# Pooling and gating in the turned layout in the front of a decoder step

## The chip, the cores and the metric

The kernel runs on one core of a Trainium2 chip. The metric is the device time of one execution in microseconds (us). All tensors and all matmuls are float32. In the trace a float32 matmul stands as two passes, so a line that issues 24 matmuls shows 48 records.

## The reference, cut to what matters

One layer of a decoder step over 1024 prompt tokens and 64 sample tokens (8 sequences of 8), width 1024. The front of the layer is what the change touches:

```python
h = rmsnorm(x, norm1_g)
proj = h @ w_in                                   # 1024 -> u 512 | v 512 | p 512
uv = gelu(proj[..., :1024]); u, v = uv[..., :512], layernorm(uv[..., 512:])
p = proj[..., 1024:]
z = einsum('hts,bcshd->bcthd', tril(ws), v) + bs  # 4 heads, chunks of 128 tokens
ya = u * z
# 4 groups of 128 channels, windows w = 2, 4, 8, 16 over the tokens
pooled = (sum of the last w rows of p) / min(pos + 1, w) - p
yb = (pooled @ b_w[g]) * b_scale
x = x + concat(ya, yb) @ w_out
```

Behind it come a second norm, a router, and a mixture of 32 experts (top 2 of 8 in one of 4 groups), each with three matrices of 2 MB, and a last norm. The last 15 rows of p of the prompt are an output of their own.

## The kernel before

**Tiles.** The tokens are cut into nine tiles: tile 0 (called "first"), tiles 1 to 7 ("mid"), and tile 8 of 64 rows ("sample"). `pipeline` calls `step(i, cur, prev, pprev, nxt)` on every engine: step i projects, gates and pools tile i, finishes the second norm and the router's logits of tile i-1, places tile i-2 in the experts' tables, and prepares the turned input `hT` of tile i+1. Steps 2 to 6 are a hardware loop, the others are written out. Each engine runs its instructions in the order of the program, and semaphores join the engines.

**TensorE in one mid step**, in its order: two small rank products (L1166, L1167); the projections v, u and p, each 8 matmuls with `hT` stationary and 512 columns of `w_in` moving, into banks 2, 3 and 4 (L1182); z, four products over the chunk (L1193, bank 5); the pooling, for each group a product with the matrix `band` and one with `band_prev` over the tile before, kept in `ptail` (L1205, bank 6); the turn of the next tile's normed input `xn` (L1131 called from L1212, banks 0 and 1); the turn of the gated `ya` (L1131 called from L1216, bank 5); the product with `b_w` (L1221); the turn of `xn2` of the tile before (called from L1228, again banks 0 and 1, so it waits until `hT` has been taken); the first half of the output projection (L1239), the router's logits (L1247), and the second half (L1255). The first half waits for `yaT_ready` and `ybT_ready`, the two halves of the turned input `yT`.

**VectorE in a mid step**: residual adds (L908, L911), placing, two norms, the layer norm of v (L929 to L944), the gate (L953: z + bias, times u, one instruction for each head), the copy of p into `ptail` (L957), `hT` of the next tile (L822), the scaled yb half of `yT` (L964), the turned h2 (L972), and the router's choice on small tiles (L833 to L853). **ScalarE**: two squares, GELU of v and of u, the copy of p, the copy of the pooled half to `poolT` (L716), and the copy of the turned `ya` into `yT` (L720).

**Behind the front** the expert phase runs 32 blocks of 64 to 96 rows. Its up-products (L1285) are already in the form in which a piece of 64 weight columns is stationary, the turned tokens move, and two such pieces fill the two halves of the array and of the PSUM partitions; its down-products are L1306.

Of the kernel before, what the change touches and what calls it, by code (L numbers as in the profile page):

```python
# [14 lines left out]
P = 128  # L15
D = 1024
SEQ = 1024
NS = 64
DEC, DSEQ = 8, 8
T = SEQ + NS  # L20
NT = SEQ // P + 1
KD = D // P
AW = 512
# [3 lines left out]
TAIL = 32  # L27
# [20 lines left out]
NOWHERE = 1 << 14  # L48
LASTSLOT = NE * (REG - P) + NE - 1
# [25 lines left out]
def build(nc, x_prompt, x_sample, state_pool, norm1_g, w_in, a_norm_g, a_norm_b, ws_sht, bs_th,  # L75
# [4 lines left out]
    with ctx:  # L80
# [20 lines left out]
        vg, p, ya, ptail = [big[:, third + (NT + 1) * D + i * AW:third + (NT + 1) * D + (i + 1) * AW] for i in range(4)]  # L101
# [7 lines left out]
        band = bands[:, 0:AW].rearrange("p (g n) -> p g n", n=P)  # L109
        band_prev = bands[:, AW:D].rearrange("p (g n) -> p g n", n=P)  # L110

        ident = sb("ident", [P, P])
        band_first = sb("band_first", [P, GROUPS, P])
# [6 lines left out]
        bst = sb("bst", [P, HEADS])  # L120
# [3 lines left out]
        gf = sb("gf", [P, D])  # L124
        bsc = sb("bsc", [P, GROUPS])
# [59 lines left out]
        turn_int = band_first[:, 3, 0:NE].bitcast(I32)  # L185
        turn_row = sb("turn_row", [P, NE])
        slot_row, slot_int, pick = band_first[:, 0, :], band_first[:, 1, :].bitcast(I32), band_first[:, 2, :]
# [23 lines left out]
        state_moved = sem("state_moved")  # L211
# [20 lines left out]
        ptail_ready = sem("ptail_ready")  # L232
# [20 lines left out]
        p7_stored = sem("p7_stored")  # L253
# [5 lines left out]
        caps_set = sem("caps_set")  # L259
# [18 lines left out]
        turns_numbered = sem("turns_numbered")  # L278
        turn_row_made = sem("turn_row_made")
        table_late = sem("table_late")  # L280
        h2_late = sem("h2_late")
        slots_numbered = sem("slots_numbered")
# [73 lines left out]
        def _(sp):  # L356
# [26 lines left out]
            for q in range(4):  # L383
# [4 lines left out]
            load(bst[:, :], bs_th)  # L388
            load(band_first[:, :, :], c_band_first)
# [4 lines left out]
                         w_out[0, 0:AW, :].rearrange("(p k) n -> p k n", k=HEADS)).then_inc(in_wout, 16)  # L394
            sp.dma_start(wout[:, HEADS:KD, :],
                         w_out[0, AW:D, :].rearrange("(g d) n -> d g n", g=GROUPS)).then_inc(in_wout, 16)
            load_late(band[:, :, :], c_band)
            load_late(band_prev[:, :, :], c_band_prev)
# [9 lines left out]
            load_late(gf[:, :], normf_g.partition_broadcast(P))  # L408
            sp.wait_ge(zeroed, 1)
            for b in range(DEC):  # L410
# [7 lines left out]
                         state_pool[0, :, DSEQ:STATE, :]).then_inc(state_moved, 16)  # L418
# [25 lines left out]
            sp.wait_ge(p_copied, LAST)  # L444
            sp.dma_start(pool_p[0, 0], p[P - STATE:P, :]).then_inc(p7_stored, 16)
# [6 lines left out]
            sp.wait_ge(v_ready, NT)  # L452
            sp.dma_start(v_s[0].rearrange("b s c -> (b s) c"), v[0:NS, :]).then_inc(outs, 16)
            sp.wait_ge(proj_p, NT)
            for n in range(CH):
                sp.dma_start(chunk_dst(n, n), chunk_src(FIRST, n)).then_inc(chunk_in[n], 16)
            store_h2(LAST, NS)
            sp.wait_ge(outs, 16 * (DEC + 1))
# [23 lines left out]
            sp.wait_ge(yaT_done, NT)  # L482
            sp.wait_ge(ptail_ready, NT)
# [19 lines left out]
            sp.wait_ge(state_moved, 16)  # L503
# [13 lines left out]
        def _(pool):  # L517
            pool.memset(wst_s[:, :, :], 0.0).then_inc(zeroed, 1)
            pool.iota(filler.rearrange("p (q c) -> p q c", c=2), pattern=[[1, NE * REG // P], [0, 2]], base=0,
# [7 lines left out]
            pool.memset(caps[:, FIRST:NE], float(NE * CAP)).then_inc(caps_set, 1)  # L527
            for lo, hi, caps_of in CLASSES + ((FINAL, FINAL + 1, FINAL_CAPS),):
                for h in range(lo, hi):
                    for s, cap in enumerate(caps_of):  # L530
                        at = SETS * (h - 1) + s
                        pool.memset(caps[:, at:at + 1], float(NE * cap)).then_inc(caps_set, 1)
# [25 lines left out]
            for j in range(LAST):  # L558
                if j == 1:
                    pool.wait_ge(pooled, 1)  # L560
                    pool.iota(turn_int, pattern=[[1, NE]], base=0, channel_multiplier=0).then_inc(turns_numbered, 1)
                    pool.iota(slot_int.rearrange("p (i w) -> p i w", w=WAYS), pattern=[[NE, P // WAYS], [NE * P // WAYS, WAYS]],
                              base=FIRST, channel_multiplier=0).then_inc(slots_numbered, 1)
# [17 lines left out]
            pool.wait_ge(filled, 9)  # L581
# [833 lines left out]
```

## Time and profile before

| | |
|---|---|
| median of 3 runs | 977.61 us (976.02 to 978.34) |
| profiled execution, its own time | 981.23 us |
| its span | 979.6 us |
| TensorE busy over the span | 900.6 us, 92% |
| VectorE busy | 257.5 us, 26% |
| ScalarE busy | 110.0 us, 11% |
| mean granted TensorE clock | 0.963 of full |

The front takes about 380 us of the span, the experts run from about 404 us to 943 us, and the last norm follows. Busy time says which engine works most; which one ends last at a given place has to be read from the order of the records there.

### The profile page before, as it was taken

What the parts mean: (1) busy time and instruction counts of PE and PEld (TensorE: products, weight loads), DVE (VectorE), ACT (ScalarE), POOL (GpSimd) and SP (SyncE); (2) the same over time, 40 slices, a digit from 0 to 9 for tenths busy, and PEclk for the clock granted to TensorE, in tenths of its full rate; (3) what the DMA queues carried; (4) which work ended last, traced back from release to release, by engine and by line L of the source; (5) the groups of instructions that cost most, each with busy time, mean ns of one, the idle gap of its engine ahead of it and who ended that gap; (6) DMA issues with size and microseconds to landing.
All of it is one profiled execution on the core that took longest, in us unless ns stands there. A gap on an engine that the chain in (4) does not pass through costs nothing.

```text
span 979.6 us, 24674 instructions
## 1 busy us (share of the span) xinstructions
PE 900.6 (92%) x10538; PEld 596.2 (61%) x10538; DVE 257.5 (26%) x779; ACT 110.0 (11%) x173; POOL 155.4 (16%) x260
## 2 busy tenths in 40 slices
PE   4999999999999995799999999999999999989940
PEld 2545555454554563767868686868686768567630
DVE  1443454625445356150010101010101010100106
ACT  0210111101111011101001000001010101001013
POOL 1000100000000000211213131312122313113110
PEclk9999999999999997699999999999999999979985
DMA  8870200201021027799999999999999999999738
GB/s 340 275 292 1 87 31 12 86 0 43 8 78 44 3 91 286 301 399 392 353 393 404 393 407 391 408 389 409 389 408 391 402 394 401 398 405 400 270 70 321
DMA packets 57440, 258.70 MB, mean 264 GB/s; under 512 B 10809, under 2 KB 11889, under 8 KB 40356
## 3 DMA queue, kind: packets, MB, share of 16 engines
q1 hardware_dynamic: 47484, 238.51, 60.7%
q0 software_dynamic: 9264, 19.36, 8.1%
q8 instruction: 41, 0.67, 0.3%
q10 hardware_dynamic: 640, 0.07, 0.1%
q14 instruction: 11, 0.09, 0.0%
HBM read 240.86 MB, written 25.04 MB: 271 GB/s over the span
## 4 chain that ended last, share of the span: by engine, by line
PE 54%; issue 3%; DVE 2%; DMA 2%; DVEq 0%; ACT 0%; SPq 0%; POOLq 0%; POOL 0%
PE ps L1285 31%; PE ps L1306 19%; PE ps L1131 3%; DVE big L1115 1%; DMA big<-x_rows 1%; DMA x_rows<-xn,sidx 0%; PE ps L1319 0%; DMA xg<-h_rows,oidx 0%; PE ps L1314 0%; DVE ssf L806 0%; DVE ssf L805 0%; DVE ssf L808 0%; DVEq L80 0%; ACT junk L784 0%; DMA slot_table<-ids,dest 0%
## 5 line engine op out<-in xcount | busy, mean ns | idle before, releaser
L1285 PEld LDWEIGHTS ps<-hT,big 128*64 128x64 f32 x8192 | 299.5, 139 | 41.1 <-issue 39.1
L1285 PE MATMUL ps<-hT,big 128*64 128x80 f32 (+2 forms) x8192 | 308.6, 236 | 13.0 <-issue 10.7
L1306 PE MATMUL ps<-big,poolT 128*80 128x512 f32 (+2 forms) x512 | 191.2, 594 | 0.6 <-issue 0.6
L1182 PE MATMUL ps<-big,hT 128*128 128x512 f32 x384 | 168.9, 599 | 4.3 <-DMA big<-in_w_in 2.9
L1182 PEld LDWEIGHTS ps<-big,hT 128*128 128x128 f32 x384 | 72.8, 192 | 95.0 <-issue 88.0
L1306 PEld LDWEIGHTS ps<-big,poolT 128*80 128x80 f32 (+2 forms) x512 | 64.5, 149 | 103.1 <-issue 102.0
L1079 DVE TENSOR_TENSOR poolT<-u,ps 128x320 f32<-128x320 f32 (+2 forms) x32 | 15.5, 486 | 421.7 <-PE ps L1285 421.7
L577 POOL DMA_INDIRECT x_rows<-xn,sidx x22 | 32.9, 1495 | 274.1 <-ACT xn L763 253.1
L553 POOL DMA_INDIRECT slot_table<-ids,dest x18 | 18.9, 1052 | 305.4 <-DVE dest L879 263.3
L1239 PE MATMUL ps<-big 128*128 128x512 f32 x128 | 56.4, 593 | 0.9 <-DVE big L964 0.9
L1255 PE MATMUL ps<-big 128*128 128x512 f32 x128 | 57.0, 598 | 0.0
L763 ACT ACTIVATE xn<-ps,gslot 80x1024 f32<-80x1024 f32 (+1 forms) x21 | 23.3, 1110 | 259.1 <-PE ps L1306 259.1
L1239 PEld LDWEIGHTS ps<-big 128*128 128x128 f32 x128 | 23.7, 190 | 28.0 <-issue 27.8
L1255 PEld LDWEIGHTS ps<-big 128*128 128x128 f32 x128 | 23.7, 190 | 27.6 <-issue 27.3
L572 POOL DMA_INDIRECT gslot<-gate_rows,pidx x32 | 32.2, 1007 | 21.3 <-POOL sidx L623 14.0
L996 DVE TENSOR_TENSOR hT<-ps,g2t 128x768 f32<-128x768 f32 (+1 forms) x32 | 28.0, 875 | 27.6 <-PE ps L1131 18.3
L1131 PE MATMUL ps<-ident,xn 128*128 128x128 f32 (+1 forms) x144 | 21.3, 297 | 13.2 <-DVE xn L817 8.4
L577 POOL DMA_INDIRECT x_rows<-bands,sidx x10 | 14.6, 1460 | 89.2 <-DVE bands L1086 76.0
L754 ACT ACTIVATE u<-ps 128x320 f32<-128x320 f32 (+2 forms) x32 | 13.9, 435 | 125.2 <-PE ps L1285 125.2
L1131 PEld LDWEIGHTS ps<-ident,xn 128*128 128x128 f32 (+1 forms) x144 | 18.6, 196 | 14.5 <-issue 9.6
L953 DVE SCALAR_TENSOR_TENSOR big<-ps,bst,u 128x128 f32<-128x128 f32 x32 | 9.0, 345 | 67.6 <-PE ps L1193 67.6
L695 ACT ACTIVATE xn<-big 128x1024 f32 (+2 forms) x9 | 9.5, 1057 | 150.3 <-DVE big L911 150.3
(184 smaller groups left out, 561.2 us busy)
## 6 DMA issues: line engine op xcount, KB each, us to landing
big<-in_exp_w SPq DMA_DIRECT2D x192, 1024.0 KB
big<-in_w_in SPq DMA_DIRECT2D x4, 1536.0 KB, 13.4
big<-in_w_out SPq DMA_DIRECT2D x2, 2048.0 KB, 14.4
x_rows<-big SPq DMA_DIRECT2D x8, 512.0 KB
h_rows<-xn SPq DMA_DIRECT2D x8, 512.0 KB, 2.9
big<-x_rows SPq DMA_DIRECT2D x8, 512.0 KB, 7.2
out_y_prompt<-big SPq DMA_DIRECT2D x8, 512.0 KB, 2.8
big<-in_x_prompt SPq DMA_DIRECT2D x1, 3072.0 KB, 11.3
```

Source lines behind the costliest of these rows:

```text
L553: pool.indirect_dma_start(slot_table, bass.IndirectOffsetOnAxis(ap=dest[0:m, j, c:c + 1], axis=0), ids[0:m, j, c, :], None, bounds_check=N ...
L572: pool.indirect_dma_start(dst, None, gate_rows, bass.IndirectOffsetOnAxis(ap=idx.bitcast(U32), axis=0), bounds_check=last_pair, oob_is_err ...
L577: pool.indirect_dma_start(x3_rows, bass.IndirectOffsetOnAxis(ap=idx.bitcast(U32), axis=0), src, None, bounds_check=last_row, oob_is_err=Tr ...
L763: act.activation(ys[s][0:m, :], ps[0:m, 5:7, :].rearrange("p a n -> p (a n)"), ACT.Copy, scale=gslot[s][0:m, 0:1]).then_inc(y_ready, 1)
L996: dve.tensor_tensor(xT[:, :, 0:ways * i].rearrange("p k (w i) -> p k w i", i=i), wide.rearrange("p k (i w) -> p k w i", w=WAYS)[:, :, 0:wa ...
L1079: dve.tensor_tensor(hhT[:, :, 0:m], s1T[:, :, 0:m], up3[:, :, 0:m], ALU.mult).then_inc(hhT_ready, 1)
L1131: last = pe.transpose(ps[:, bank + c // 4, (c % 4) * P:(c % 4) * P + m], xs[:, c, :], ident[0:m, 0:m])
L1182: last = pe.matmul(ps[0:m, bank, :], hT[:, k, 0:m], win[:, k, part * AW:(part + 1) * AW], start=(k == 0), stop=(k == KD - 1))
L1239: last = pe.matmul(ps[0:m, 6, :], yT[:, k, 0:m], wout[:, k, 0:512], start=(k == 0), stop=(k == KD - 1))
L1255: last = pe.matmul(ps[0:m, 7, :], yT[:, k, 0:m], wout[:, k, 512:D], start=(k == 0), stop=(k == KD - 1))
L1285: last = pe.matmul(out[c * w:(c + 1) * w, j, 0:m], up_weights(n)[:, k, j * P + c * w:j * P + (c + 1) * w], xT[:, 4 * half + k, 0:m], start ...
L1306: last = pe.matmul(ps[first:first + m, 5 + cols, :], hhT[:, 2 * half + k, 0:m], down_weights(n)[:, k, cols * 512:(cols + 1) * 512], start= ...
```

## The change

- u and p of tiles 0 to 7 are projected turned: 64 columns of `w_in` are stationary and the 128 tokens of `hT` move, two such pieces side by side (`SPLIT` is 2). The order is now v, p, u.
- ScalarE copies the turned p into `pT`, which has 16 columns of the tile before (`HALO`) ahead of its 128. VectorE forms sums over 2, 4, 8 and 16 tokens by four adds along the free axis, then `poolT` from them. The products with `band`, `band_prev` and `band_first` are gone, and the copies L716 and L957 with them.
- z is computed turned (v stationary, the chunk matrix moving), its bias lies along the free axis and is loaded as a broadcast row, and VectorE writes the gated product straight into `yT`. The turn of `ya` and the copy L720 are gone. The rows of `w_out` of this half are loaded in another order to fit.
- Tile 0 has extra VectorE work: the shares 1/min(pos+1, w), the bias laid out anew, and five small instructions that mend its first 16 columns.
- At step 7 four small products turn back the last 16 rows of p for the output.
- The sample tile keeps the old form. The load of `gf` moves from the start to behind the last mid tile; three 256 KB loads of band matrices are gone and a 256 KB bias broadcast is new. Some semaphores are merged, and `hT` now also waits for `proj_u`.

```diff
+            def pool_tile(i, first):
+                at = lambda t, lo, by=0, gs=slice(0, GROUPS): t[:, gs, lo - by:HALO + P - by]
+                dve.wait_ge(p_copied, i + 1)
+                reached(dve, yb_done, i)
+                dve.tensor_tensor(at(sum2, 2), at(pT, 2), at(pT, 2, 1), ALU.add).then_inc(sum_step, 1)
+                dve.wait_ge(sum_step, 4 * i + 1)
+                dve.tensor_tensor(at(sum4, 4, 0, slice(0, 3)), at(sum2, 4, 0, slice(1, 4)), at(sum2, 4, 2, slice(1, 4)), ALU.add)\
+                    .then_inc(sum_step, 1)
...
+                for g, w in enumerate(WINDOWS):
+                    last = dve.scalar_tensor_tensor(poolT[:, g, :], sums[g][:, HALO:], 1.0 / w, pT[:, g, HALO:],
+                                                    ALU.mult, ALU.subtract)
+                if first:
...
+                last.then_inc(poolT_ready, 1)
+                dve.tensor_copy(pT[:, :, 0:HALO], pT[:, :, P:HALO + P]).then_inc(halo_ready, 1)
...
+                if isinstance(i, int) and i == 0:
+                    dve.wait_ge(in_small, 16 * len(small))
+                    dve.tensor_copy(bias[:, :, :], bias_in.rearrange("p (t h) -> p h t", h=HEADS)).then_inc(share_step, 1)
...
+                if cur and cur != "sample":
+                    pool_tile(i, cur == "first")
+                    dve.wait_ge(z_done, i + 1)
+                    dve.tensor_tensor(ya[:, :], ps[:, 5, :], bias.rearrange("p h n -> p (h n)"), ALU.add).then_inc(z_biased, 1)
+                    dve.wait_ge(z_biased, i + 1)
+                    dve.wait_ge(u_gelu, i + 1)
+                    reached(dve, out_b, i)
+                    dve.tensor_tensor(yT[:, 0:HEADS, :], ya.rearrange("p (h n) -> p h n", n=P),
+                                      u.rearrange("p (h n) -> p h n", n=P), ALU.mult).then_inc(yaT_ready, 1)
...
+                        for bank, part, free, done in ((4, 2, p_copied, proj_p), (3, 0, u_gelu, proj_u)):
+                            reached(pe, free, i)
+                            for j in range(AW // P):
+                                for k in range(KD):
+                                    for c in range(SPLIT):
+                                        at = part * AW + j * P + c * NS
+                                        last = pe.matmul(ps[c * NS:(c + 1) * NS, bank, j * P:(j + 1) * P],
+                                                         win[:, k, at:at + NS], hT[:, k, :], start=(k == 0),
+                                                         stop=(k == KD - 1), skip_group_check=True)
+                            last.then_inc(done, 1)
...
-                    for g in range(GROUPS):
-                        for n, (src, bnd, kk) in enumerate(parts):
-                            for c in range(P // w):
-                                last = pe.matmul(ps[c * w:(c + 1) * w, 6, g * P:g * P + m],
...
-                    pe.wait_ge(ya_ready, i + 1)
-                    turn(ya, m, yaT_done, HEADS, 5)
+                    if cur == "sample":
+                        pe.wait_ge(ya_ready, 1)
+                        turn(ya, m, yaT_done, HEADS, 5, whole=True)
                     pe.wait_ge(poolT_ready, i + 1)
```

TensorE's part of one step of the loop (tiles 2 to 6) before the change, in its order:

```order
L1182 MATMUL ps<-big,hT 128x512 x24
L1193 MATMUL ps<-v,done_early 128x128 x4
L1205 MATMUL ps<-bands,big 128x128 x8
L1210 REGISTER_ALU
L1131 MATMUL ps<-ident,xn 128x128 x8
L1131 MATMUL ps<-ident,big 128x128 x4
L1221 MATMUL ps<-poolT,done_early 128x128 x4
L1131 MATMUL ps<-ident,xn 128x128 x8
L1239 MATMUL ps<-big 128x512 x8
```

The same part after the change (L1249 is v, L1258 is p and then u, L1274 is z, L1199 the turns, L1308 the product with `b_w`, L1326 the first half of the output):

```order
L1249 MATMUL ps<-big,hT 128x512 x8
L1258 MATMUL ps<-hT,big 64x128 x128
L1274 MATMUL ps<-done_early,v 128x128 x4
L1295 REGISTER_ALU
L1199 MATMUL ps<-ident,xn 128x128 x8
L1308 MATMUL ps<-poolT,done_early 128x128 x4
L1199 MATMUL ps<-ident,xn 128x128 x8
L1326 MATMUL ps<-big 128x512 x8
```

Sixteen wide projection matmuls have become 128 narrow ones, and the eight band products and the four turns of `ya` are gone; between z and the output only turns and the product with `b_w` are left.

VectorE from the end of v to the turned h2 of a mid tile before the change (step 1):

```order
L944 TENSOR_TENSOR v<-v,done_early 128x512
L953 SCALAR_TENSOR_TENSOR big<-ps,bst,u 128x128 x4
L957 COPY big<-big 128x512
L822 TENSOR_TENSOR hT<-ps,g1t 128x1024
L964 TENSOR_TENSOR big<-ps,bsc 128x512
L972 TENSOR_TENSOR done_early<-ps,g2t 128x1024
```

And after it, in the same step (L906 to L914 are the four adds, L919 forms `poolT`, L930 keeps the halo, L1010 adds the bias, L1014 multiplies by u into `yT`, L842 is `hT`, L1031 the yb half):

```order
L1002 TENSOR_TENSOR v<-v,done_early 128x512
L906 TENSOR_TENSOR big<-bands 128x4x142
L908 TENSOR_TENSOR bands<-big 128x3x140
L911 TENSOR_TENSOR big<-bands 128x2x136
L914 TENSOR_TENSOR bands<-big 128x128
L919 SCALAR_TENSOR_TENSOR poolT<-big,bands 128x128
L919 SCALAR_TENSOR_TENSOR poolT<-bands 128x128
L930 COPY bands<-bands 128x4x16
L1010 TENSOR_TENSOR big<-ps,gf 128x512
L1014 TENSOR_TENSOR big<-big,u 128x512
L842 TENSOR_TENSOR hT<-ps,g1t 128x1024
L1031 TENSOR_TENSOR big<-ps,bsc 128x512
```

The pooling stands ahead of the gate in VectorE's order, and the gate has become two instructions of 512 elements, both ahead of `hT`. (L919 stands four times in the program; the two forms alternate.)

## Rows read from the trace of the kernel before

**Rows 1.** The page: busy time by engine, and the granted clock in 40 slices.
```profile
PE 900.6 (92%) x10538; PEld 596.2 (61%) x10538; DVE 257.5 (26%) x779; ACT 110.0 (11%) x173; POOL 155.4 (16%) x260
...
PEclk9999999999999997699999999999999999979985
```
**Rows 2.** Timeline of TensorE, one mid tile (start, length, records, idle before).
```profile
183.05 20.85 PE L1182 MATMUL ps<-big,hT 128*128 128x512 f32 x48
203.74 1.05 PE L1193 MATMUL ps<-v,done_early 128*128 128x128 f32 x8
204.63 2.01 PE L1205 MATMUL ps<-bands,big 128*128 128x128 f32 x16
206.47 1.05 PE L1131 MATMUL ps<-ident,xn 128*128 128x128 f32 x8
207.36 0.65 PE L1131 MATMUL ps<-ident,big 128*128 128x128 f32 x4
207.84 1.06 PE L1221 MATMUL ps<-poolT,done_early 128*128 128x128 f32 x8
208.93 1.13 PE L1131 MATMUL ps<-ident,xn 128*128 128x128 f32 x8
209.90 7.03 PE L1239 MATMUL ps<-big 128*128 128x512 f32 x16
```
**Rows 3.** Timeline of VectorE in the same tile.
```profile
194.88 0.69 DVE L944 TENSOR_TENSOR v<-v,done_early 128x512 f32<-128x512 f32 x1
204.83 1.13 DVE L953 SCALAR_TENSOR_TENSOR big<-ps,bst,u 128x128 f32<-128x128 f32 x4 [9.26 <-PE ps L1193]
...
207.56 1.22 DVE L822 TENSOR_TENSOR hT<-ps,g1t 128x1024 f32<-128x1024 f32 x1 [0.46 <-PE ps L1131]
208.94 0.69 DVE L964 TENSOR_TENSOR big<-ps,bsc 128x512 f32<-128x512 f32 x1 [0.15 <-PE ps L1221]
```
**Rows 4.** Timeline of ScalarE in the same tile.
```profile
203.94 0.60 ACT L679 ACTIVATE big<-ps 128x512 f32<-128x512 f32 x1 [6.27 <-PE ps L1182]
```
**Rows 5.** Timeline of TensorE in the expert phase, a block of 96 rows.
```profile
610.95 10.73 PE L1285 MATMUL ps<-hT,big 128*64 128x96 f32 x256
621.61 1.16 PE L1131 MATMUL ps<-ident,xg 128*128 128x128 f32 x8
622.60 7.03 PE L1306 MATMUL ps<-big,poolT 128*96 128x512 f32 x16
```
**Rows 6.** Timeline of TensorE, projections of the sample tile.
```profile
352.23 10.58 PE L1144 MATMUL ps<-big,hT 128*64 128x256 f32 x96
```
**Rows 7.** VectorE's groups by form, a small operation (count, busy us, mean ns).
```profile
L843 DVE TENSOR_TENSOR rm<-rm,ra 128x32 f32<-128x32 f32 x4 | 0.8, 191 | 0.1
```
**Rows 8.** Timeline of TensorE, tile 7.
```profile
330.34 1.05 PE L1193 MATMUL ps<-v,done_early 128*128 128x128 f32 x8
...
336.71 7.10 PE L1239 MATMUL ps<-big 128*128 128x512 f32 x16
```
**Rows 9.** Timeline of TensorE, tile 0.
```profile
37.58 1.05 PE L1193 MATMUL ps<-v,done_early 128*128 128x128 f32 x8
...
42.72 7.10 PE L1239 MATMUL ps<-big 128*128 128x512 f32 x16 [0.88 <-DVE big L964]
```
**Rows 10.** Timeline of VectorE, tile 0.
```profile
35.01 0.69 DVE L944 TENSOR_TENSOR v<-v,done_early 128x512 f32<-128x512 f32 x1
...
39.71 0.42 DVE L957 COPY big<-big 128x512 f32<-128x512 f32 x1
```
**Rows 11.** Busy us by stretch: PE, PEld, DVE, ACT, POOL, then clock, DMA share.
```profile
38.00:42.00 4.00, 3.85 (x34) 3.65 (x32) 2.80 (x7) 1.57 (x3) 0.00 (x0) 1.00 0.94 231
...
363.00:366.00 3.00, 3.00 (x42) 2.37 (x40) 1.21 (x5) 0.71 (x3) 0.00 (x0) 1.00 0.10 19
...
367.00:370.00 3.00, 3.00 (x18) 1.94 (x16) 1.24 (x2) 0.00 (x0) 0.00 (x0) 0.50 0.65 118
...
386.00:388.00 2.00, 0.63 (x6) 0.49 (x5) 1.15 (x6) 0.00 (x0) 0.00 (x0) 0.50 0.19 68
```
**Rows 12.** Timeline of TensorE, the expert loop's first pass, block of 64 rows.
```profile
505.83 2.20 PE L1285 MATMUL ps<-hT,big 128*64 128x64 f32 x67 [0.76 <-issue]
```

More of the change, by code:

```diff
@@ L26 @@
 WINDOWS = (2, 4, 8, 16)
-TAIL = 32
+HALO = 16
 NG, NE, EPG = 4, 32, 8
@@ L100, in build @@
         yT = big[:, third + NT * D:third + (NT + 1) * D].rearrange("p (k n) -> p k n", n=P)
[L101 removed]
+        vg, ya, p, _ = [big[:, third + (NT + 1) * D + i * AW:third + (NT + 1) * D + (i + 1) * AW] for i in range(4)]
         done_early = sb("done_early", [P, D + 4 * AW])
@@ L124, in build @@
         gf = sb("gf", [P, D])
+        bias = gf[:, 0:AW].rearrange("p (h n) -> p h n", n=P)
+        share = gf[:, AW:AW + GROUPS * HALO].rearrange("p (g n) -> p g n", n=HALO)
         bsc = sb("bsc", [P, GROUPS])
@@ L1126, in _, with turn @@
         def _(pe):
-            def turn(x, m, done, k=KD, bank=0):
-                xs = x[0:m, :].rearrange("t (p k) -> t k p", k=k)
+            def turn(x, m, done, k=KD, bank=0, whole=False):
+                xs = x[0:m, :].rearrange("t (k p) -> t k p" if whole else "t (p k) -> t k p", k=k)
                 for c in range(k):
@@ L1192, in step @@
                     for h in range(HEADS):
-                        last = pe.matmul(ps[0:m, 5, h * P:(h + 1) * P], w[0:m, h, 0:m],
-                                         v[0:m, h * P:(h + 1) * P], start=True, stop=True)
-                    last.then_inc(z_done, 1)
-                    pe.wait_ge(p_copied, i + 1)
-                    reached(pe, ptail_ready, i)
-                    reached(pe, x2a_ready, i)
-                    parts = {"first": [(p, band_first, P)], "mid": [(p, band, P), (ptail, band_prev, P)],
-                             "sample": [(p, band_s, NS), (state, band_state, DEC * STATE)]}[cur]
@@ L1208, in step @@
-                    last.then_inc(pooled, 1)
+                        if cur == "sample":
+                            last = pe.matmul(ps[0:m, 5, h * P:(h + 1) * P], w[0:m, h, 0:m],
+                                             v[0:m, h * P:(h + 1) * P], start=True, stop=True)
+                        else:
+                            last = pe.matmul(ps[:, 5, h * P:(h + 1) * P], v[:, h * P:(h + 1) * P], w[:, h, :],
+                                             start=True, stop=True)
+                    last.then_inc(z_done, 1)
@@ new lines, in step @@
+                    if isinstance(i, int) and i == LAST - 1:
+                        pe.wait_ge(p_copied, i + 1)
+                        for g in range(GROUPS):
+                            last = pe.matmul(ps[0:HALO, 4, g * P:(g + 1) * P], pT[:, g, P:HALO + P], ident[:, :],
+                                             start=True, stop=True, skip_group_check=True)
+                        last.then_inc(rows_turned, 1)
+                    if cur == "sample":
+                        pe.wait_ge(p_copied, i + 1)
+                        pe.wait_ge(x2a_ready, i)
+                        w = P // SPLIT
+                        for g in range(GROUPS):
+                            for n, (src, bnd, kk) in enumerate(((p, band_s, NS), (state, band_state, DEC * STATE))):
+                                for c in range(P // w):
+                                    last = pe.matmul(ps[c * w:(c + 1) * w, 6, g * P:g * P + m],
+                                                     src[0:kk, g * P + c * w:g * P + (c + 1) * w], bnd[0:kk, g, 0:m],
+                                                     start=(n == 0), stop=(n == 1), skip_group_check=True)
+                        last.then_inc(pooled, 1)
```

191 lines of the change are left out of this document (113 added, 78 removed).

## The prediction

> **What bounds the kernel now.** I read the page first: TensorE is busy 92% of the span, VectorE 26%, and the clock is full except around the end of the front and of the kernel [rows 1]. Then the timeline of one mid tile on three engines. On TensorE the records of a mid tile follow each other with no idle time at all: projections from 183.05, z at 203.74, and the output's first half at 209.90 [rows 2]. VectorE meanwhile stands idle 9.26 us before the gate [rows 3], and ScalarE 6.27 us before its copy of p [rows 4]. So in the front TensorE's own work is the period of a tile, and whatever leaves it is worth its full time only until another engine ends later. I call T the start of z; everything is counted from it: z starts at T, the output's first half at T + 6.16 (209.90 - 203.74) [rows 2].
>
> **Removed from TensorE.** The band products take 206.47 - 204.63 = 1.84 us, the turn of `ya` 207.84 - 207.36 = 0.48 us, together 2.32 us a mid tile [rows 2]. In tile 0 the band products are half as many (0.92). That is the offer, not the gain.
>
> **The turned projections.** Before, 48 records take 203.74 - 183.05 = 20.69 us, 431 ns each; u and p are 32 of them, 13.79 us [rows 2]. After, u and p are 128 matmuls, 256 records, in pairs on the two halves of the array: 128 pairs of 128 columns. The nearest row is the expert block with 96 columns in the same form: 256 records in 621.61 - 610.95 = 10.66 us, 83.3 ns a pair [rows 5]. A column of a wide matmul costs 431/512 = 0.84 ns, so 32 more columns make 110.2 ns. The lower bound is pure streaming, 128 x 0.84 = 107.8 ns, the upper one the sample tile, where 96 records of 256 columns take 10.58 us, 220 ns a pair [rows 6]: less 128 x 0.84 that is 112.6 ns. I take 110 ns, the nearest form: 14.08 us, so +0.29 (from 0 to +0.6). The array changes between full and half width twice more a tile. Behind L1285 the eight turns take 622.60 - 621.61 = 0.99 us where they take 207.36 - 206.47 = 0.89 us in the front [rows 5, 2], so such a change costs at most 0.1; I take 0.15 for both (0 to 0.2). T comes 0.44 us later in each tile.
>
> **From T to the output: VectorE's chain.** Now VectorE decides. The gate started 204.83 - 203.74 = 1.09 us behind T [rows 3, 2]; z is as long as before. The bias add and the product with u are 512 elements each, 0.69 as L944 and L964 [rows 3], with some 0.03 between: they end at T + 2.51. u must have its GELU by T + 1.8: ScalarE starts 203.94 - 203.74 = 0.20 behind the projections' end and takes 0.60 [rows 4, 2], done at T + 0.8, so the new place of u as the last projection costs nothing. `hT` needs the turn of `xn`, which runs from T + 0.89 and is taken 207.56 - 206.47 = 1.09 later [rows 2, 3], T + 1.98: VectorE is later. `hT` is then T + 2.55 to T + 3.77 (1.22 long), the yb half T + 3.80 to T + 4.49. TensorE's turn of `xn2` waits for `hT`, as the two share banks: before, it began 208.93 - (207.56 + 1.22) = 0.15 behind it, and the output started 0.97 later [rows 2, 3]. So the output starts at T + 3.92 + 0.97 = T + 4.89, against T + 6.16: -1.27 us. Of the 2.32 us offered 1.05 turn into idle time of TensorE between the product with `b_w` and the turn of `xn2`.
>
> **The pooling on VectorE is hidden.** v is ready at 195.57, 8.2 us before T [rows 3]. p is projected second, so its copy lands about T - 7.04 + 0.8 = T - 6.2. The four adds have 568, 420, 272 and 128 elements; from 0.69 for 512 and 0.19 for 32 [rows 3, 7] an element costs 1.04 ns above a base of 0.16: 0.75 + 0.60 + 0.44 + 0.29 = 2.1. Four products of 128 cost 1.13 as L953 does [rows 3], the halo copy 0.2, gaps 0.15: 3.6 us, ending at T - 2.6. It would have to double (3.7 us of cover until T + 1.09) to show; beyond that each us costs a us in each tile.
>
> **Mid tiles:** 0.44 - 1.27 = -0.83, times 7 = -5.8 us. Tile 7 started its output at T + 6.37 (336.71 - 330.34) [rows 8]; the four products that turn p's rows back (8 records, 0.9 as z's eight) stand inside the lull: `xn` is turned by T + 2.9, `hT` of 64 columns by T + 3.6, the product with `b_w` ends near T + 3.9 and the output starts near T + 4.75. That is 0.35 better than counted: -0.35.
>
> **Tile 0** loses. v is ready at 35.70 only [rows 10], since the second input tile is late, and z comes at 37.58 [rows 9], so the cover is 3 us, not 9.3. Behind 35.70 stand the bias copy (0.42 as L957, up to 0.7 as it is strided) [rows 10], the 3.4 us of adds and products, four products and a difference on 16 columns (5 x 0.19 [rows 7]) and the halo: VectorE is free at about 41.0, not at 39.1. Then 0.69 + 0.69 + 1.22 + 0.69 and gaps, and TensorE starts the output at 44.6 against 42.72 [rows 9]: +1.9 (+1.2 to +2.5).
>
> **Nothing else is counted.** The sample tile keeps its instructions. The gf load, 0.5 MB, now stands ahead of the six expert loads; at 400 GB/s that is 1.3 us later for data first used at 404 us, and the DMA engines are nearly empty (share 0.19) at 386 to 388 us [rows 11]. Without that slack it would cost the 1.3 us. The loads saved at the start feed nothing that TensorE waits for. GpSimd's new wait for the small outputs stands behind transfers long finished.
>
> **Sum:** -5.8 - 0.35 + 1.9 = -4.25 us. The profiled execution has 981.23 us of its own time (span 979.6 and 1.6 around it), so 977.0; it lies 3.6 above the median of 977.61, and against the median the forecast is 973.4.
>
> **Rivals.**
>
> *The narrow pairs are slower than I think.* For: 256-column pairs of the sample tile cost 220 ns, 5 ns over streaming, and 256 weight loads a tile must hide. Against: at 96 columns, with less time to hide a load, the pair is 2.7 ns over streaming [rows 5]. Each ns is 128 x 8 = 1.0 us, so 114 ns a pair would make the change worth nothing: 977.6. Chance 0.13. The Trainium skill has a rule that speaks for this, in "TensorE: Matmul & The Clock Gate", section "Back-to-back issue gap": a sustained stream of weight loads and matmuls needs about 81 ns for 128 columns where the isolated gap is 56. If 25 ns a pair were added here, an estimate by that page, the time would be near 999; the trace does not show such a surplus in any row of this form.
>
> *The clock falls in the lull, which ends slower.* After T there are now turns, 0.9 us of products with `b_w` and 1.05 us of idle time. In the sample tile the clock dropped to 0.50 of full, 1.2 GHz, in 367 to 370 us, though TensorE was busy the whole 3.00 us in 363 to 366, with small tiles only [rows 11]; so busy time alone does not hold it. Three us at half speed cost 1.5 us. At every one of eight tiles: +12 - 4.25, 985.4; three such falls cancel the gain. Against: tile 0 of before had turns, one group of products and 0.88 us idle in a row [rows 9], and the clock stayed 1.00 [rows 11]. Chance 0.15 for three or more. The Trainium skill says in the same page, section "Part 4: PE-mode transpose", that turns do not count as busy for the clock; by that rule the lull holds 0.9 us of counted work and the removed band products were what kept it up. The trace has no place that tells this.
>
> *First passes through longer code stall.* TensorE's code of a step doubles. The expert loop's first pass shows 0.76 us of "issue" idle time [rows 12]. Four first passes (tiles 0, 1, 2, 7) at 0.5 to 0.8 give back 2 to 3 us: 976. Chance 0.1.
>
> *More comes back.* Pairs at 107.8 ns, no cost of changing width, tile 0 at +1.2: -4.25 - 2.3 - 1.2 - 0.7 = -8.4, 969.2. If VectorE's chain hid all, 7 x 2.32 would be -16; nothing supports that, since the chain of four dependent operations is made of measured pieces. Chance 0.08.
>
> **How the numbers follow.** My forecast, 971.5 to 975.6, has 0.54; more gain 0.08; stalls 0.1; slow pairs 0.13; clock 0.15. A measurement of this kernel tells about 0.2%, 2 us, from no change. The forecast and the larger gain are faster (0.62) and half of the stalls (0.05); the slow pairs are half no change, a quarter on each side; the clock case is slower in four of five. That makes faster 0.70, same 0.13, slower 0.17. The range from 968.5 to 980.5 leaves out about 2 in 10.
>
> **What would show it.** L1258 with 256 records in 14.0 to 14.2 us; output start at z + 4.9 with about 1 us idle before the turn of `xn2`, released by `hT`; a period of 32.3 us in place of 33.15; tile 0's output at 44.6. I am wrong if the 256 records take over 14.6 us, if the clock leaves 1.00 between 40 and 360 us, or if the four adds take over 3 us.

## The result and the profile after

The changed kernel takes 983.55 us (median of 4, 981.15 to 984.51), the kernel before 977.98 us beside it (976.02 to 978.57): ratio 1.0057, interval 1.0038 to 1.0076. It is slower, by 0.6%; the forecast was 973.4. Ratios, here and below, leave out executions over 1.5% above the same kernel's fastest, while medians and ranges are those of all executions, so where times come in steps the range tells more. The profiled execution took 981.15 us, the lowest of the four; its span is 979.4, against 979.6 for the profiled one of before, which lay 3.6 us above its kernel's median. So this pair of profiles ends together, and shows what was gained and what was lost, but not the whole of the 5.6 us between the medians.

The page of the changed kernel, busy time by engine and the granted clock in 40 slices (against [rows 1]):

```profile
PE 888.5 (91%) x12186; PEld 641.1 (65%) x12186; DVE 280.8 (29%) x838; ACT 100.9 (10%) x158; POOL 155.3 (16%) x262
...
PEclk9999999999999996899999899999999999999985
```

TensorE has 12.1 us less work. A new notch in its clock stands in the slice from 539 to 563 us, in the middle of the experts; the kernel before has one there too, later, in its slice from 857 to 882 us. First the mid tile of [rows 2] and [rows 3]; the timeline of TensorE:

```profile
188.75 14.20 PE L1258 MATMUL ps<-hT,big 128*64 128x128 f32 x256
202.88 1.16 PE L1274 MATMUL ps<-done_early,v 128*128 128x128 f32 x8
203.87 1.04 PE L1199 MATMUL ps<-ident,xn 128*128 128x128 f32 x8
204.75 1.06 PE L1308 MATMUL ps<-poolT,done_early 128*128 128x128 f32 x8
206.77 1.14 PE L1199 MATMUL ps<-ident,xn 128*128 128x128 f32 x8 [0.96 <-DVE hT L842]
207.74 7.03 PE L1326 MATMUL ps<-big 128*128 128x512 f32 x16
```

The timeline of VectorE in the same tile:

```profile
196.63 0.75 DVE L906 TENSOR_TENSOR big<-bands 128x568 f32<-128x568 f32 x1 [2.40 <-ACT bands L718]
197.42 0.60 DVE L908 TENSOR_TENSOR bands<-big 128x420 f32<-128x420 f32 x1
198.05 0.44 DVE L911 TENSOR_TENSOR big<-bands 128x272 f32<-128x272 f32 x1
198.53 0.29 DVE L914 TENSOR_TENSOR bands<-big 128x128 f32<-128x128 f32 x1
...
199.67 0.19 DVE L930 COPY bands<-bands 128x64 f32<-128x64 f32 x1
204.07 0.69 DVE L1010 TENSOR_TENSOR big<-ps,gf 128x512 f32<-128x512 f32 x1 [4.21 <-PE ps L1274]
204.80 0.69 DVE L1014 TENSOR_TENSOR big<-big,u 128x512 f32<-128x512 f32 x1
205.41 1.22 DVE L842 TENSOR_TENSOR hT<-ps,g1t 128x1024 f32<-128x1024 f32 x1
```

The output starts 4.86 us behind z, and 0.96 us of TensorE's time waits for `hT`. The mid tiles are as forecast. In tile 7, in the timeline of TensorE,

```profile
327.04 1.16 PE L1274 MATMUL ps<-done_early,v 128*128 128x128 f32 x8
...
332.16 7.10 PE L1326 MATMUL ps<-big 128*128 128x512 f32 x16
```

the output starts at 332.16 where [rows 8] have 336.71: the front had gained 4.55 us. The first expert product starts at 397.39, before at 404.11: 6.7 us. The 2.2 us more are not the change's for certain: 1.6 of them lie between tile 7's output and the last rank product (52.96 us here, 54.53 before), and the kernel before takes 53.03 there in e2 and e3 below.

By the end of the experts nothing of it is left. The timeline of TensorE where the changed kernel goes round its first expert loop (a pass is three blocks, of 96, 80 and 64 rows; an ordinary one takes 49.0 us):

```profile
551.46 3.65 PE L1393 MATMUL ps<-big,poolT 128*64 128x512 f32 x16
559.08 4.10 PE L1372 MATMUL ps<-hT,big 128*64 128x96 f32 x47 [3.97 <-issue]
564.58 10.30 PE L1372 MATMUL ps<-hT,big 128*64 128x96 f32 x209 [1.41 <-issue]
...
609.61 0.34 PE L1372 MATMUL ps<-hT,big 128*64 128x64 f32 x4 [1.18 <-issue]
...
614.45 1.74 PE L1372 MATMUL ps<-hT,big 128*64 128x96 f32 x38
```

And busy us, clock and DMA share by stretch there:

```profile
552.00:555.00 3.00, 3.00 (x16) 1.00 1.05 429
555.00:558.00 3.00, 0.11 (x2) 0.91 1.01 396
558.00:561.00 3.00, 1.92 (x24) 0.50 1.01 423
561.00:566.00 5.00, 3.59 (x46) 0.50 1.02 354
566.00:569.00 3.00, 3.00 (x57) 0.72 1.03 417
```

TensorE stops for 4 us with nothing to wait for ("issue"), and its clock falls to 0.50 (1.2 GHz) for about 10 us: the pass from 555.0 to 614.5 takes 10.5 us more than an ordinary one. 6.6 us of that are the three idle stretches shown (3.97, 1.41 and 1.18); the other 3.9 fit the work done at half clock. It happens again at 666 (+8.4, 5.9 of it idle). The kernel before has one such place, in its second loop, about 10 us over an ordinary pass; its timeline of TensorE (the second record goes on behind the window):

```profile
857.83 2.11 PE L1285 MATMUL ps<-hT,big 128*64 128x80 f32 x33 [2.73 <-issue]
862.93 3.36 PE L1285 MATMUL ps<-hT,big 128*64 128x80 f32 x47 [2.98 <-issue]
```

From the first up-product to the last down-product the experts take 535.5 us before (404.11 to 939.59) and 542.6 after (397.39 to 939.94). The DMA view has a queue named instruction, whose packets are 16 KB each. In 520 to 740 us (inside the first loop) it says for the changed kernel

```profile
q8 instruction: 18, 0.29, 0.6%
```

and has no such line for the kernel before; in 740 to 880 us before has 12 of these packets, after 7. So it looks as if TensorE's instructions were fetched a second time in the middle of a loop (I call that a refetch); that the packets are TensorE's is borne out below, where moving TensorE's loops alone moves them.

### The profile page after: what moved, and what is told of

It reads as the page before. It is cut to its first block and busy times, and to the rows that moved or that the text cites. A ratio compares the mean times of both kernels' runs of the same rounds, so it can differ in the third digit from the quotient of the medians.

```text
span 979.4 us, 28026 instructions
## 1 busy us (share of the span) xinstructions
PE 888.5 (91%) x12186; PEld 641.1 (65%) x12186; DVE 280.8 (29%) x838; ACT 100.9 (10%) x158; POOL 155.3 (16%) x262
## 5 line engine op out<-in xcount | busy, mean ns | idle before, releaser
L1372 PEld LDWEIGHTS ps<-hT,big 128*64 128x64 f32 x8192 | 300.1, 139 | 47.1 <-issue 44.7
L1258 PEld LDWEIGHTS ps<-hT,big 128*64 128x64 f32 x2048 | 111.6, 137 | 6.1 <-issue 6.1
L1258 PE MATMUL ps<-hT,big 128*64 128x128 f32 x2048 | 113.6, 273 | 0.0
L1249 PE MATMUL ps<-big,hT 128*128 128x512 f32 x128 | 58.9, 611 | 4.2 <-DMA big<-in_w_in 2.8
L1326 PE MATMUL ps<-big 128*128 128x512 f32 x128 | 56.4, 593 | 2.1 <-DVE big L1031 2.1
L1249 PEld LDWEIGHTS ps<-big,hT 128*128 128x128 f32 x128 | 24.3, 195 | 33.4 <-issue 26.7
L1326 PEld LDWEIGHTS ps<-big 128*128 128x128 f32 x128 | 23.7, 190 | 29.2 <-issue 29.0
L1199 PE MATMUL ps<-ident,xn 128*128 128x128 f32 (+1 forms) x144 | 20.5, 289 | 18.6 <-DVE xn L836 8.3
L1199 PEld LDWEIGHTS ps<-ident,xn 128*128 128x128 f32 (+1 forms) x144 | 18.0, 194 | 20.0 <-issue 15.2
```

What stands on the lines that cost most here:

```text
L1199: last = pe.transpose(ps[:, bank + c // 4, (c % 4) * P:(c % 4) * P + m], xs[:, c, :], ident[0:m, 0:m])
L1249: last = pe.matmul(ps[:, 2, :], hT[:, k, :], win[:, k, AW:2 * AW], start=(k == 0), stop=(k == KD - 1))
L1258: last = pe.matmul(ps[c * NS:(c + 1) * NS, bank, j * P:(j + 1) * P], win[:, k, at:at + NS], hT[:, k, :], start=(k == 0), stop=(k == KD - 1 ...
L1326: last = pe.matmul(ps[0:m, 6, :], yT[:, k, 0:m], wout[:, k, 0:512], start=(k == 0), stop=(k == KD - 1))
L1372: last = pe.matmul(out[c * w:(c + 1) * w, j, 0:m], up_weights(n)[:, k, j * P + c * w:j * P + (c + 1) * w], xT[:, 4 * half + k, 0:m], start ...
```

## The experiments

Theory A: TensorE keeps a limited number of 16 KB blocks of its program, and the place of a loop in the code decides how many blocks its body touches. Counted in the compiled programs (a slot is one instruction; a float32 matmul is 4 slots, two weight loads and two passes, a turn 2, a block 256), the body of an expert pass has 1693 slots, 6.6 blocks: 7 or 8, by its start. It touches 7 blocks when it starts at slot 0 to 99 of a block. The change lengthens TensorE's code ahead of the loops by 1666 slots, 6 blocks and 130 slots, so both loops start elsewhere. The start slots given in e15 and e16 for the two kernels as they are come from this count; a few slots more or less would leave the number of blocks as it is. Rival B: the transfers of weights bind the experts. Rival C: spells of slow transfers by chance.

**Placement (e1 to e6, e13, e15, e16).** One edit, with a pair of start slots for the two loops:

```diff
-            for lo, hi, caps_of in CLASSES:
-                with eng.Fori(lo, hi) as h:
+            for (lo, hi, caps_of), slot in zip(CLASSES, (0, 0)):
+                with nc.Fori(lo, hi, engines=OrderedEngineSet([eng.engine]),
+                             head_slot={eng.engine: slot} if eng.engine == mybir.EngineType.PE else None) as h:
```

e1. 

> Both expert loops of TensorE's program start at the first slot of an instruction block (a fetched block is one 16 KB packet of the queue named instruction); the loop body then lies in 7 such blocks. Nothing else differs from the changed kernel. Theory A (the loop's place in the code decides whether its instructions are fetched again): the two long passes of the changed kernel (59.3 and 57.2 us where the others take 49.1) become ordinary ones, no instruction packet lies inside a later pass of either loop, and up to 10.2 + 8.1 = 18 us come back; since the kernel before had one such pass too, the ratio to it should be about 0.98 to 0.993. Theory B (the expert phase is bound by its weight transfers and ends when they end, whatever the front does): the end stays within 2 us of the changed kernel's, ratio about 1.004 to 1.007. Theory C (chance spells of slow transfers): long passes remain, at other places.

e2. 

> The same placement in the kernel before. Theory A: its one long pass (57.4 us, the last but one of the second loop) becomes an ordinary one, up to 8 us come back, ratio 0.991 to 0.995, and the changed kernel with the same placement is faster than this one by what its front gained, about 6.7 us (0.7%). Theory B: no change, ratio 0.998 to 1.002. Theory C: no change within the scatter, with a long pass at some other place.

e3. 

> The kernel before with both expert loops at slot 160 of a block, so that the body lies in 8 blocks, in both loops. Theory A: instruction packets appear in later passes of the first loop as well, with long passes of some 57 to 59 us; 8 to 20 us slower than the kernel before, ratio 1.008 to 1.02, although nothing of the computation differs. Theories B and C: ratio 0.998 to 1.002.

e4. 

> The changed kernel with both expert loops at slot 160 of a block (8 blocks for the body, as the first loop has where the changed kernel leaves it). Theory A: the two long passes of the first loop stay and one may be added in the second, as the kernel before has there: ratio 1.005 to 1.018, and at least 12 us slower than the same kernel with slot 0. Theories B and C: the same time as with slot 0, within 2 us.

e5. 

> The loop body counts 1693 slots of 1792 in 7 blocks, so it fits into 7 from any start slot up to 99. Here both loops start at slot 96. Theory A (what decides is the number of blocks that the body touches): as with slot 0, no instruction packet inside a later pass of either loop, ratio to the kernel before 0.983 to 0.990. Rival D (what helps is that the head of the loop stands at the start of a block): long passes come back, ratio 1.005 or more.

e6. 

> Both loops eight slots further on, at 104, so that the last five slots of the body lie in an eighth block. Theory A: instruction packets in later passes, two or three long ones, ratio 1.005 to 1.019, some 20 us over slot 96 for eight slots. If the count of slots is off by a few, it equals slot 96. Rival D: the same as slot 96.

e13. 

> The changed kernel as it is, once more. Theory A: in it the first loop lies in 8 blocks, so instruction packets appear in its later passes in some or all executions; times in steps of some 10 us, the lowest near slot 0's (960 to 967), the median near the first result's ratio, 1.003 to 1.010. If the loss is one of a single chip, the ratio is 0.993 as with slot 96.

e15. 

> The changed kernel with the placement of the kernel before: first loop at slot 32 (7 blocks), second at slot 192 (8 blocks). Theory A: no refetch in the first loop, at times one in the second; faster than before by its front, about 4 us (ratio 0.991 to 0.998), which is what was forecast for the change. Otherwise as the changed kernel, 1.004 to 1.008.

e16. 

> The kernel before with the placement of the changed kernel: first loop at slot 160 (8 blocks), second at slot 64 (7 blocks). Theory A: long passes in the first loop, none in the second, 5 to 12 us slower than the kernel before (ratio 1.005 to 1.012), and about 4 us slower than the changed kernel. Otherwise 0.998 to 1.002.

Measured; "packets" are those of the instruction queue in 520 to 740 and 740 to 880 us (7 of the second number are there in the profiles of this table without a refetch, from the first pass of loop 2; a refetch that lies across 740 or 880 us has some of its packets on the other side), "stops" the refetches seen in the one profile of each run.

| kernel, slots | chip | packets | stops | us, median (range) | ratio to before |
|---|---|---|---|---|---|
| e1 after, 0 and 0 | 3 | 0, 7 | 0 | 966.98 (963.3 to 970.3) | 0.986 (0.984 to 0.988) |
| e2 before, 0 and 0 | 3 | 0, 7 | 0 | 970.46 (967.8 to 971.5) | 0.990 (0.989 to 0.992) |
| e3 before, 160 and 160 | 3 | 18, 9 | 3 | 992.73 (980.8 to 1001.8) | 1.009 (1.006 to 1.011) |
| e4 after, 160 and 160 | 3 | 14, 11 | 2 | 990.53 (988.3 to 1001.3) | 1.015 (1.010 to 1.019) |
| e5 after, 96 and 96 | 1 | 0, 7 | 0 | 962.24 (960.1 to 966.3) | 0.993 (0.991 to 0.995) |
| e6 after, 104 and 104 | 1 | 0, 14 | 1 | 977.25 (963.4 to 989.2) | 0.999 (0.996 to 1.003) |
| e13 after, as it is | 10 | 9, 7 | 1 | 983.84 (976.1 to 989.5) | 1.005 (1.003 to 1.008) |
| e15 after, 32 and 192 | 10 | 0, 20 | 2 | 987.34 (985.5 to 988.2) | 1.011 (1.009 to 1.012) |
| e16 before, 160 and 64 | 10 | 14, 11 | 2 | 987.41 (976.2 to 992.5) | 1.009 (1.006 to 1.012) |

The first expert blocks of e16, the kernel before with nothing changed but its loops' place, in the timeline of TensorE, and e1's at the same place:

```profile
564.13 3.84 PE L1287 MATMUL ps<-hT,big 128*64 128x96 f32 x46 [2.82 <-issue]
569.53 5.50 PE L1287 MATMUL ps<-hT,big 128*64 128x96 f32 x128 [1.56 <-issue]
...
613.72 0.34 PE L1287 MATMUL ps<-hT,big 128*64 128x64 f32 x5 [1.08 <-issue]
```
```profile
559.73 10.73 PE L1374 MATMUL ps<-hT,big 128*64 128x96 f32 x256
```

The signature of the changed kernel (a stop behind the branch, another about 47 records on, one near the end of the pass) can be put into the kernel before and taken out of the changed one. With start slots 0, 32, 64 and 96 no refetch is seen in any loop; with 104, 160 and 192 there is one or more in some loop of each run, though not in every such loop (e6's first had none). Eight slots, 96 to 104, cost 15 us at the median. How many refetches an execution has is left to chance: two profiles of the changed kernel as it is show two (the first, 981.15 us) and one (e13, 976.34 us). e6's times lie near 965, 976 and 986 us, but which number of refetches makes which step is not shown: its profiled execution, with one, took 967.35 us.

B falls as the cause: with the same transfers the medians lie 15 to 24 us apart. But it has a part on the chips of e5 to e12, whose passes are shorter: there the kernels without a refetch wait for weights near the end of the second loop, 2.3 us in e5, 2.7 in e12 and 4.7 in e9. Out of e12's timeline of TensorE:

```profile
886.93 1.94 PE L1395 MATMUL ps<-big,poolT 128*64 128x512 f32 x8 [1.14 <-DMA big<-in_exp_w]
889.82 1.94 PE L1395 MATMUL ps<-big,poolT 128*64 128x512 f32 x8 [0.95 <-DMA big<-in_exp_w]
```

e6, held up by its refetch, has no such wait, so that its experts end only 4.5 us behind e5's (929.13 and 924.62). On those chips a part of what the front gains is lost to this wait. C falls as the cause of the difference; chance only decides in which pass a loop of eight blocks is fetched again, and how often. The other guess that e5 was to test, that the loop's head must stand at the start of a block, falls with slot 96.

Several expectations missed. e6's ratio, 0.996 to 1.003, lies below 1.005 to 1.019, while the median of all its executions is at 1.008. e15 refetched twice in its second loop where the kernel before did once, and so was slower, not faster, than it. e5's ratio is above 0.983 to 0.990, on another chip than e1. e2's is 0.990 for 0.991 to 0.995, and e1 is 3.5 us under it, not 6.7. e13's fastest, 976.07, is nowhere near 960 to 967.

In e1 and e2 no loop is refetched, and the ends differ by the front alone: 3.5 us, and the forecast was 4.25. By the same pairs a refetch-free placement is worth 9.3 us to the kernel before (979.8 to 970.5 on one chip) and some 17 to the changed one (983.6 or 983.8 as it is to 967.0, on different chips). An estimate from these, 17 - 9.3 - 3.5 = 4, is near the 5.6 us by which the change lost.

The Trainium skill has the blocks: "Runtime: NRT & Kernel Launch", section "Instruction fetch mechanics", gives TensorE 128 KiB in 16 KiB blocks, which makes eight; the threshold between 7 and 8 blocks fits, if one is the block fetched ahead (that is a guess; no run shows it). The same section says that a taken branch out of a window of two pages forces a fetch. By that every back-edge of a seven-block body would stop; the trace shows none of them stopping (five passes of e5's first loop take 47.76 or 47.77 us each), and the measurement decides.

**The hint (e12, e14).** The loops where they fall, but the loop tells TensorE's fetch that its branch goes back:

```diff
+                with nc.Fori(lo, hi, engines=OrderedEngineSet([eng.engine]),
+                             hint_back_edge=(eng.engine == mybir.EngineType.PE)) as h:
```

e12. 

> The changed kernel with the loops where they fall and a hint to TensorE's instruction fetch that the branch at the end of the body goes back. If the cost lies in the block of the loop's head being asked for only at the branch, the long passes shrink, and 5 to 15 us come back. If the blocks were dropped because there are too many of them, the packets and the long passes stay: ratio as for the changed kernel, 1.000 to 1.012.

e14. 

> The changed kernel with the hint on the back edge, on the same chip as the changed kernel as it is. If the hint cures it: 0.986 to 0.997, some 10 us under the other. If not: the same as the other.

e12: 966.13 us (963.2 to 968.0), ratio 0.997 (0.995 to 0.998). e14: 970.79 us (969.5 to 972.9), ratio 0.994 (0.992 to 0.996), beside e13's 983.84 on the same chip. No packet inside the first loop, no refetch in either loop, 13 us back, though by the count the first loop still touches eight blocks (the hint adds one slot to a body). So eight blocks alone do not force a refetch: theory A is right about the place, but a lack of room for eight blocks cannot be the whole cause. e12's second alternative, too many blocks, falls with that; what the fetch does at the end of the body stays open. The hint has a price where the loop is left. Behind e12's second loop the timeline of TensorE has

```profile
898.35 10.39 PE L1374 MATMUL ps<-hT,big 128*64 128x80 f32 x238 [5.07 <-issue]
```

and e14 stops for 1.76 and 1.54 us at the same place; e1 has 0.43 there. Of the two cures the pinned slot gives more: 0.993 (e5) against 0.997 (e12), on chips where the kernel before takes the same 969.2 us.

**The pooling twice (e7)** and **the bias twice (e8)**, with slots 0:

```diff
...
+                for n in range(8):
+                    dve.tensor_tensor(*adds[n // 2], ALU.add).then_inc(sum_step, 1)
+                    dve.wait_ge(sum_step, 8 * i + n + 1)
```
```diff
+                    for n in range(2):
+                        dve.tensor_tensor(ya[:, :], ps[:, 5, :], bias.rearrange("p h n -> p (h n)"), ALU.add).then_inc(z_biased, 1)
+                        dve.wait_ge(z_biased, 2 * i + n + 1)
```

e7. 

> Slot 0, and each of the four running-sum additions of the pooling is done twice, 2.1 us more on VectorE per tile, the result unchanged. If the pooling is hidden in a mid tile, as predicted (its last operation ends 3.0 us before z begins), the period of a mid tile stays 41.4 us, and only tile 0 is later by 2.1 us: ratio to before 0.986 to 0.992, and 1 to 3 us over slot 0 alone. If VectorE sets the step, the period grows to 43.5 us and the time by 17 us.

e8. 

> Slot 0, and the addition of the bias to z is done twice, 0.69 us more between z and the product with w_out. If this chain sets the end of a step, as predicted, the first output product comes 5.55 us behind z in place of 4.86, the period of a mid tile is 42.1 us in place of 41.4, and the eight tiles cost 5.5 us: ratio to before 0.989 to 0.994. If TensorE's own work set it, nothing changes.

e7: 965.80 us, ratio 0.997 (0.996 to 0.998); e8: 968.80, ratio 1.000 (0.999 to 1.001), both on the chip of e5 (0.993). The second adds run from 201.67 to 206.08 in e7 and TensorE's mid tile does not notice them: out of its timeline

```profile
207.91 1.16 PE L1272 MATMUL ps<-done_early,v 128*128 128x128 f32 x8
...
211.81 1.13 PE L1197 MATMUL ps<-ident,xn 128*128 128x128 f32 x8 [0.96 <-DVE hT L844]
212.78 3.60 PE L1324 MATMUL ps<-big 128*128 128x512 f32 x8
```

T + 4.87, period 41.39 as without. In e8's timeline the wait for `hT` grows by all of the 0.73 us, and the period is 42.11:

```profile
208.95 1.16 PE L1277 MATMUL ps<-done_early,v 128*128 128x128 f32 x8
...
213.57 1.13 PE L1202 MATMUL ps<-ident,xn 128*128 128x128 f32 x8 [1.69 <-DVE hT L844]
214.54 4.03 PE L1329 MATMUL ps<-big 128*128 128x512 f32 x9
```

The expected ratios missed, mostly since slot 0 was taken from e1's chip (0.986). Against e5 (slot 96, no refetch either) the costs are 3.6 us for e7 (1 to 3 expected) and 6.6 for e8 (5.5 expected), about 1 us too much each. Both profiles show the clock falling behind tile 0, which e5's does not; e7's first output half takes 9.33 us there where e5's takes 7.10, and that would cover the surplus. Busy us, clock and DMA share of e7 there:

```profile
40.00:43.00 3.00, 0.70 (x7) 1.00 0.13 35
43.00:46.00 3.00, 1.28 (x8) 0.71 0.03 1
46.00:49.00 3.00, 2.36 (x3) 0.50 0.88 232
49.00:52.00 3.00, 3.00 (x6) 0.65 1.02 419
```

**Tile 0 in another order (e9), a shorter chain (e10), both (e11)**, all with slots 0. In e9 `square1(1)` on ScalarE and `norm1(1)` on VectorE stand behind the GELU and the layer norm of v of tile 0. In e10:

```diff
                     w = wst_s if cur == "sample" else wst
+                    # ahead of z: the turn of xn
+                    turn(xn, m_of(nxt), xT_done)
...
                     pool_tile(i, cur == "first")
+                    take_hT(i + 1, m_of(nxt))
                     dve.wait_ge(z_done, i + 1)
...
+                        for g in range(GROUPS):     # ScalarE, in place of L1031
+                            last = act.activation(yT[:, HEADS + g, :], ps[:, 6, g * P:(g + 1) * P], ACT.Copy,
+                                                  scale=bsc[:, g:g + 1])
```

e9. 

> Slot 0, and in tile 0 alone ScalarE takes gelu(v) before it squares x of tile 1, and VectorE normalizes v before x of tile 1 (the load of x of tile 1 holds both up). The pooling should then end before z, so that TensorE no longer waits 0.9 us for poolT, and the first output product comes at about 42.3 to 43 us in place of 43.8 to 44.7. TensorE's idle time there shrinks from 3 us to under 2; if this lull is what drops its clock in some executions (0.50 for about 3.4 us behind 45 us), the drop goes too, and the first period is 41 us. 1 to 3 us under slot 0 alone. If it isn't the lull, the drop stays in some executions.

e10. 

> Slot 0, and a shorter chain in tiles 0 to 7: x of the next tile is turned ahead of z, hT is taken before the gate, and ScalarE takes the scaled yb in four pieces in place of VectorE. Between z and the output TensorE has b_w and one turn left (T+3.2 or so with T the start of z, which itself starts 1.0 us later), so about T+4.1 to T+4.3 by the old T in place of 4.86: period 40.6 to 40.8 in place of 41.4, 4 to 5.5 us less than slot 0 alone. If ScalarE's four pieces take over 1.5 us, the gain falls to under 3 us.

e11. 

> Both edits and slot 0 together: 5 to 8 us under slot 0 alone, ratio to before 0.978 to 0.988, whatever the chip.

e9: 961.39 us, ratio 0.992 (0.990 to 0.993). Tile 0 in its timeline of TensorE:

```profile
38.28 1.16 PE L1285 MATMUL ps<-done_early,v 128*128 128x128 f32 x8
39.28 1.05 PE L1210 MATMUL ps<-ident,xn 128*128 128x128 f32 x8
40.16 1.06 PE L1319 MATMUL ps<-poolT,done_early 128*128 128x128 f32 x8
42.78 7.11 PE L1337 MATMUL ps<-big 128*128 128x512 f32 x16 [1.56 <-DVE big L1042]
```

The wait for `poolT` is gone and the output starts at 42.78, 1.8 us earlier than in e5; in the total this is 0.9 us, not the 1 to 3 expected, and hardly told from e5 (962.24, 0.993); the longer wait for weights in e9 (4.7 us against 2.3) may hold the rest. In the profiles without this edit the clock fell behind tile 0's lull in 9 of 12 (the exceptions are the first one, e5 and e6), in those with it in 0 of 2, in those of the kernel before and its placements in 0 of 4. Counts, not a proof; but the lull of 3 us (0.91 ahead of `b_w`, 2.09 ahead of the output) belongs to the change, where before had 0.88.

e10: 958.16 us, ratio 0.989 (0.987 to 0.991), 4.1 us under e5, on another chip on which the kernel before takes the same 969.2. The mid tile in its timeline of TensorE:

```profile
204.95 1.16 PE L1210 MATMUL ps<-ident,xn 128*128 128x128 f32 x8
205.95 1.06 PE L1289 MATMUL ps<-done_early,v 128*128 128x128 f32 x8
206.84 1.06 PE L1323 MATMUL ps<-poolT,done_early 128*128 128x128 f32 x8
207.73 1.05 PE L1210 MATMUL ps<-ident,xn 128*128 128x128 f32 x8
209.22 7.10 PE L1341 MATMUL ps<-big 128*128 128x512 f32 x16 [0.44 <-ACT big L730]
```

The output starts 4.27 us behind the projections in place of 4.86, and the period is 40.87: 0.52 less, not the 0.6 to 0.8 expected, because ScalarE's four pieces end last now, by 0.44 us. e11: 956.98 us (956.2 to 958.0), ratio 0.9875 (0.986 to 0.989), 5.3 us under e5 as expected: the best version here, faster than both kernels.

## Why the prediction was wrong

- **The turned projections** held: 202.88 - 188.75 = 14.13 us against 14.08, 110.4 ns a pair. The 25 ns more by the rule of the Trainium skill ("TensorE: Matmul & The Clock Gate", section "Back-to-back issue gap") were not there.
- **The chain** held: T + 4.86 against T + 4.89, `hT` the releaser of 0.96 us, and e8 shows that what is added to it adds to the period in full (0.73 us).
- **The hidden pooling** held: its adds are 0.75, 0.60, 0.44 and 0.29 as worked out, and it ends at T - 3.0; e7 shows them hidden at twice their length.
- **Mid tiles** held: -0.83 forecast; from tile 4 to tile 7 a tile took (330.34 - 203.74) / 3 = 42.20 us before [rows 2, 8] and (327.04 - 202.88) / 3 = 41.39 after, -0.81. The "period of 32.3 in place of 33.15" in the list of signs was a slip: these are no periods.
- **Tile 7** was off: T + 5.12, not T + 4.75. The rows turned back stand ahead of the turn of `xn`, and TensorE's own work there fills the whole lull.
- **Tile 0** held in place (44.53 and 44.71 in e5 and e1, forecast 44.6; 43.82 in the first profile). The rival of the falling clock came true at this one tile, in 9 of 12 profiles though not in that of the result, and nowhere at the six others with 0.96 us of idle: from 60 to 345 us the clock is 1.00 in every profile.
- **The sum for the front** held: -4.25 forecast, -4.55 at tile 7's output in the first profile, in part by luck, since tile 0 came 0.8 us earlier than forecast there and tile 7 0.37 later. From tile 0's z to tile 7's output the kernel before takes 299.13 us in all four of its profiles, the changed one 294.54 in the first and 294.38 in e5; in e1, where the clock fell behind tile 0, it takes 295.94, and e1 ends 3.5 us under e2.
- **"Nothing else is counted" is the step that failed.** TensorE's code ahead of the experts grew, and moved loops whose instructions were not touched. By the count the first loop went from 7 blocks to 8, and paid two refetches (18.9 us in the profile), and the second from 8 to 7, and saved one (about 10). The front's gain was paid back by the experts, which the sum had at nothing. The rival of longer code was at the right engine, but priced as 0.5 to 0.8 us at first passes, from a row of the first pass [rows 12]; that a later pass could stop was in no row of the first loop. It was in the trace, though: the second loop of before stops in front of 857.83 and again in front of 862.93, and [rows 1] have the mark of it, a 7 in the clock of the slice from 857 to 882 us. The prediction read those slices as full except around the end of the front and of the kernel, which is wrong. The sum took every pass to be like the one of [rows 5].
- Open: by what rule blocks are dropped, why the passes with a refetch vary, and why the hint keeps eight blocks.

## What to carry to other kernels

Where a change lengthens or shortens an engine's code ahead of a loop, count the slots: find the loop's start and how many blocks its body touches before and after, for float32 matmuls weigh four. List the length of every pass of a loop, and look at the instruction queue's packets inside it: a packet behind the first pass is a refetch, and here each made its pass 8 to 12 us longer. Pin the loop's start, or give its back-edge the hint (which cost up to 5 us where the loop is left), before timing anything smaller than that.

## What the hardware showed unexpectedly

- A stop of 2.7 to 4 us of TensorE in the middle of dense work cost more than twice its length: there were two or three more stops in the same pass, and a clock at 0.50, for about 10 us at 558 in the changed kernel and at 858 in the one before, for about 3 at 667.
- Whether a loop of eight blocks is refetched differs between executions of one program: e6 took 963.4 to 989.2 us, and two profiles of the changed kernel show two refetches and one.
- At full clock the same pass took 49.14 us in e1 and 47.77 in e5, on another chip. The difference is in the pairs of narrow blocks (80 rows: 9.37 and 9.07 us; 64 rows: 8.8 and 7.68), not in those of 96 (10.73 in both). Ten such passes would account for most of the difference by which the kernel before took 979.8 us on one chip and 969.2 on another, but on the second it was not profiled; the cause is open.
